# Triangular inverses in a gated delta rule: the second form of each level's inverse made by transposition

## The reference, cut to what matters

```python
L = jnp.where(strict, jnp.einsum('bhncd,bhnsd->bhncs', k_beta, k) * decay, 0.0)
A = jnp.eye(C, dtype=f32) + L
u = lax.linalg.triangular_solve(A, v * beta[..., None], left_side=True, lower=True, unit_diagonal=True)
w = lax.linalg.triangular_solve(A, k_beta * jnp.exp(gc)[..., None], left_side=True, lower=True, unit_diagonal=True)
```

## Time and profile before

| | us |
|---|---|
| median of 3 runs | 4347.78 |
| lowest, highest | 4346.86, 4359.89 |
| the profiled execution | 4345.83 |
| its span, first to last instruction | 4344.0 |
| mean granted TensorE clock | 0.966 of full |

### The profile page before, as it was taken

The page is one execution under the profiler, slowest core; times in us unless marked ns, Lnnn a source line. Parts: engine busy times, 40 slices in busy tenths (PEclk is TensorE's granted clock), DMA queues, the critical chain, the costliest instruction groups (busy, mean ns, idle before and its releaser), DMA issues.

```text
span 4344.0 us, 36733 instructions
## 1 busy us (share of the span) xinstructions
PE 4066.7 (94%) x13837; PEld 2293.4 (53%) x13837; DVE 2045.6 (47%) x3759; ACT 869.9 (20%) x1735; POOL 390.1 (9%) x252
## 2 busy tenths in 40 slices
PE   6998989999999999998998999989998969599999
PEld 3343555555554555544445444456664458556665
DVE  2130530898104456564323298046665055455666
ACT  2111520000113111113133000221112131242111
POOL 1110000344020000000000034100000000100000
PEclk9999999999999999999999999999999979589999
DMA  5552001111112111111210222122222200102222
GB/s 209 194 204 68 1 9 55 58 39 58 39 64 63 59 58 58 58 57 43 78 39 5 78 78 78 58 107 78 97 78 75 69 20 0 48 1 78 97 78 78
DMA packets 124950, 294.51 MB, mean 68 GB/s; under 512 B 5130, under 2 KB 13370, under 8 KB 124800
## 3 DMA queue, kind: packets, MB, share of 16 engines
q1 hardware_dynamic: 107824, 236.58, 15.4%
q0 software_dynamic: 16976, 55.84, 3.8%
HBM read 290.23 MB, written 2.18 MB: 67 GB/s over the span
## 4 chain that ended last, share of the span: by engine, by line
PE 87%; DVE 6%; ACT 3%; DMA 2%; issue 1%; POOL 0%; DVEq 0%; SPq 0%; ACTq 0%
PE psum L357 30%; PE psum L1911 29%; PE psum L1970 14%; PE psum L1905 3%; PE psum L2015 2%; PE psum L1998 1%; DMA sb_rc<-in_ada_b 1%; ACT sb_rc L1670 1%; PE psum L1956 1%; DMA sb_ring<-in_ada_w 1%; PE psum L1021 1%; ACT sb_rb L1670 1%; PE psum L1034 1%; PE psum L1035 1%; PE psum L1999 0%
## 5 line engine op out<-in xcount | busy, mean ns | idle before, releaser
L1911 PE MATMUL psum<-sb_ht,sb_ring 128*128 128x512 f32 (+1 forms) x2448 | 891.7, 526 | 3.7 <-DVE sb_kvt L2298 2.1
L1911 PEld LDWEIGHTS psum<-sb_ht,sb_ring 128*128 128x128 f32 x2448 | 464.0, 190 | 431.2 <-issue 409.9
L2286 DVE SCALAR_TENSOR_TENSOR sb_rc<-sb_rc,sb_vec x960 | 475.6, 572 | 0.0
L1970 PE MATMUL psum<-sb_ring,sb_ht 128*128 128x512 f32 (+1 forms) x1088 | 466.2, 590 | 5.3 <-DVE sb_rc L2330 3.6
L1670 ACT ACTIVATE sb_rc<-psum 128x512 f32<-128x512 f32 (+2 forms) x330 | 167.3, 525 | 1159.1 <-DVE sb_ra L519 308.1
L357 PE MATMUL psum<-sb_ring,sb_rc 128*128 128x512 f32 x868 | 391.8, 593 | 7.5 <-DVE sb_rc L503 7.5
L1970 PEld LDWEIGHTS psum<-sb_ring,sb_ht 128*128 128x128 f32 x1088 | 208.3, 193 | 262.2 <-issue 256.9
L357 PE MATMUL psum<-sb_ht,sb_ring 128*128 128x256 f32 (+1 forms) x1152 | 306.6, 416 | 0.0
L1670 ACT ACTIVATE sb_kvt<-psum 128x512 f32<-128x512 f32 (+2 forms) x197 | 100.0, 533 | 1004.6 <-PE psum L1911 788.0
L1911 PE MATMUL psum<-sb_rc,sb_ring 128*128 128x512 f32 (+1 forms) x768 | 276.6, 522 | 4.3 <-ACT sb_rc L1670 2.5
L357 PEld LDWEIGHTS psum<-sb_ring,sb_rc 128*128 128x128 f32 x868 | 164.5, 190 | 216.6 <-issue 204.3
(11 more groups left out here) (358 smaller groups left out, 4486.1 us busy)
## 6 DMA issues: line engine op xcount, KB each, us to landing
sb_ring<-in_w_in SPq DMA_DIRECT2D x37, 2048.0 KB, 8.0
sb_ring<-in_w_ff SPq DMA_DIRECT2D x32, 2048.0 KB, 8.0
sb_rc<-in_ada_w POOLq DMA_DIRECT2D x20, 2048.0 KB, 8.3
sb_ring<-in_w_ffn SPq DMA_DIRECT2D x16, 2048.0 KB, 7.9
sb_ring<-in_w_out SPq DMA_DIRECT2D x6, 2048.0 KB, 8.1
sb_ring<-in_ada_w SPq DMA_DIRECT2D x4, 2048.0 KB, 12.9
sb_ring<-in_w_gmlp_o SPq DMA_DIRECT2D x4, 2048.0 KB, 8.3
sb_ring<-in_w_attn_o SPq DMA_DIRECT2D x4, 2048.0 KB, 7.9
```

The costliest lines, as they stand in the source:

```text
L1911: last = pe.matmul(bank(b + v, m), ring[:, slot, k, j * P:(j + 1) * P], rhs[:, k, a:a + m], start=k == 0, stop=k == KT - 1)
L1970: last = pe.matmul(bank(4 + g % 4, width), lhs[:, k, i * P:(i + 1) * P], ring[:, slot, k, 0:width], start=k == 0, stop=k == KT - 1)
L2286: step = stt(conv_slot(j, a, m), conv_slot(j + 1, a + k, m), vec[:, j, k:k + 1], conv_slot(j, a, m), op0=ALU.mult, op1=ALU.add)
```

## The change

TensorE no longer makes `xi` by a product. It makes `xit` alone (3 matmuls a unit), and when VectorE has subtracted it, TensorE transposes the new `xit` of the unit before (`turn_back`, 3 transpositions into bank 5 + u % 3, semaphore `s_xt_ps`) and ScalarE copies the result to `xi` (`turned`). The count `s_x0` becomes `s_x_cm` with 40 counts, 8 from the start values and 8 for each of four levels, and the first product of a unit waits for its own unit's count. In the last level nothing is transposed; that level stands outside the loop on TensorE and ScalarE. The waits at the end of each level are gone; VectorE waits once for its own last subtraction, behind the loop.

```diff
-            with act.Fori(0, 5) as level:
-                for u in range(8):
+            def level_evictions(level, last_level):
+
+                def first(u):
                     act.wait_ge(*s_p1_ps.at(0, 8 * level + u + 1))
                     fn(lm[:, u, :, :], bank(u % 2, 384).rearrange("p (h n) -> p h n", h=3)).then_inc(s_p1_sb.sem, 1)
+
+                def turned(u):
+                    act.wait_ge(*s_xt_ps.at(0, 8 * level + u + 1))
+                    fn(xi[:, u, :, :], bank(5 + u % 3, 384).rearrange("p (h n) -> p h n", h=3)).then_inc(s_x_cm.sem, 1)
+
+                first(0)
+                first(1)
+                for u in range(8):
+                    if u + 2 < 8:
+                        first(u + 2)
+                    if u and not last_level:
+                        turned(u - 1)
+                if not last_level:
+                    turned(7)
+
+            with act.Fori(0, 4) as level:
+                level_evictions(level, False)
+            level_evictions(4, True)
...
-            with pe.Fori(0, 5) as level:
+            def level_products(level, last_level):
+
                 def first(u):
                     pe.wait_ge(*s_bt.at(0, 8 * level + u + 1))
+                    pe.wait_ge(*s_x_cm.at(0, 8 * level + u + 1))
                     if u >= 2:
                         pe.wait_ge(*s_p1_sb.at(0, 8 * level + u - 1))
...
+                def turn_back(u):
+                    pe.wait_ge(*s_xx_sb.at(0, 8 * level + u + 1))
+                    pe.wait_ge(*s_x_cm.at(0, 8 * level + u + 6))
+                    for h in range(3):
+                        last = turn(bank(5 + u % 3, P, h * P), xit[:, u, h, :])
+                    last.then_inc(s_xt_ps.sem, 1)
...
-                        pe.matmul(bank(2 + u % 3, P, h * P), xit[:, u, h, :], lm[:, u, h, :], start=True, stop=True)
-                        last = pe.matmul(bank(5 + u % 3, P, h * P), lm[:, u, h, :], xit[:, u, h, :],
+                        last = pe.matmul(bank(2 + u % 3, P, h * P), lm[:, u, h, :], xit[:, u, h, :],
                                          start=True, stop=True)
                     last.then_inc(s_xx_ps.sem, 1)
-                pe.wait_ge(*s_xx_sb.at(0, 8 * level + 8))
+                    if u and not last_level:
+                        turn_back(u - 1)
+                if not last_level:
+                    turn_back(7)
+
+            with pe.Fori(0, 4) as level:
+                level_products(level, False)
+            level_products(4, True)
...
                     dve.wait_ge(*s_xx_ps.at(0, 8 * level + u + 1))
-                    ch_x = tt(xi[:, u, :, :], xi[:, u, :, :], bank(2 + u % 3, 384).rearrange("p (h n) -> p h n", h=3),
-                              ALU.subtract)
-                    tt(xit[:, u, :, :], xit[:, u, :, :], bank(5 + u % 3, 384).rearrange("p (h n) -> p h n", h=3),
+                    tt(xit[:, u, :, :], xit[:, u, :, :], bank(2 + u % 3, 384).rearrange("p (h n) -> p h n", h=3),
                            ALU.subtract).then_inc(s_xx_sb.sem, 1)
-                dve.wait_ge(*s_xx_sb.at(0, 8 * level + 8))
-
+
+            dve.wait_ge(*s_xx_sb.at(0, 40))
             dve.wait_ge(*s_p1_ps.at(0, 40))
```

More of the change, by code:

```diff
@@ L658, in build_program @@
         s_lt_sb = signal("lt_sb", 8)
-        s_x0 = signal("x0", 8)
+        s_x_cm = signal("x_cm", 40)
         s_bt = signal("bt", 40)
@@ L664, in build_program @@
         s_xx_sb = signal("xx_sb", 40)
+        s_xt_ps = signal("xt_ps", 32)
         s_wu_ps = signal("wu_ps", 8)
@@ L1009, in second_pe @@
             pe.wait_ge(*s_qd2.at(0, 1))
-            pe.wait_ge(*s_x0.at(0, 8))
+            pe.wait_ge(*s_x_cm.at(0, 8))
             pe.wait_ge(*s_lt_sb.at(0, 8))
@@ L1304, in second_dve @@
                 ch.note(tt(xit[:, u, :, :], rep(ident[:, :], 3), xit[:, u, :, :], ALU.subtract))
-                tt(xi[:, u, :, :], rep(ident[:, :], 3), xi[:, u, :, :], ALU.subtract).then_inc(s_x0.sem, 1)
-            dve.wait_ge(*s_x0.at(0, 8))
+                tt(xi[:, u, :, :], rep(ident[:, :], 3), xi[:, u, :, :], ALU.subtract).then_inc(s_x_cm.sem, 1)
+            dve.wait_ge(*s_x_cm.at(0, 8))
             dve.wait_ge(*s_lt_sb.at(0, 8))
```

## The result

| | before | after |
|---|---|---|
| median of 4 executions, us | 4347.57 | 4319.89 |
| lowest, highest | 4346.86, 4359.89 | 4319.34, 4321.30 |
| the profiled execution, us | 4345.83 | 4320.28 |
| its span | 4344.0 | 4318.3 |

The ratio is 0.9925, with a 95% interval from 0.9908 to 0.9942. The kernel is faster by more than 0.3%. The medians are 27.7 us apart and the two profiled spans 25.7 us; the ratio takes in the one execution of the kernel before at 4359.89 us and stands for 32.6 us (0.0075 x 4347.57).

A forecast was written before the change was run, and what follows sets the result against it. TensorE was taken to bound the kernel, busy 94% of the span. Terms 26.8 - 10.7 + 6.7 + 0.5 + 2.8 - 0.3 = 25.8 us less gave 4320.0 to 4322.0, stated as 4321 us; range 4316 to 4330.

The forecast's parts named there:

- The sum: Whole kernel: 26.8 - 10.7 + 6.7 + 0.5 + 2.8 - 0.3 = 25.8 us gained, all passed on to the end.
- The records: TensorE in the levels: 240 product records removed (26.8 us), 96 transpositions added (10.7 us), net 16.1 us less.
- changing between the two kinds of record: TensorE, between matmuls and transpositions: claimed to cost nothing where the tile stays 128x128.
- the first rival: Within units: new waits eat 10.7 us (4332), or each change of record kind costs 0.1 us (4327); together 0.12.
- The boundaries: Between levels: each costs 0.73 us beyond counted transpositions where it cost 2.41; 1.68 x 4 = 6.7 us gained.
- What is late next at the boundary is the mask product: Level boundary: after the change the VectorE mask product, not ScalarE, is late next; 1.40 us by the chain's pieces.
- The end: Before the next stage: one subtraction fewer gains 0.5 us; some 0.3 us lost if the loop exit is paid twice.
- The clock: Levels three and five: 1.4 us each lost to a lower clock after idle TensorE, 2.8 us counted as gained.
- The second rival: Levels: transpositions count as idle, the clock falls to half, 34 us slower, 4381 us; chance 0.04.
- The third rival: Later stage: a transfer or fixed event bounds it and the gain is waited away, 4346 us; chance 0.03.
- the step from the sum to the range: Whole kernel: range 4316 to 4330 us, the forecast with a few us of scatter, and the change-of-kind case.

The follow-up runs named there:

- e5_by_matmul: Changed kernel with each transposition made by an fp32 matmul with the identity, two records instead of one; levels 78.4 us, one execution 4344.14 us.
- e6_unrolled: Changed kernel with the level loops of TensorE, VectorE and ScalarE written out; levels 69.1 us, ratio 0.9940 to the kernel before.
- e8_idle: Changed kernel with five more VectorE mask products ahead of each level's first, so TensorE idles at the boundaries; levels 87.3 us.
- e2_waits: Kernel before with both products kept, the waits at each level's end replaced by waits per unit; levels 90.3 us, ratio 0.9981.
- b1_before: Kernel before, unedited, profiled again to catch a long execution; 4360.74 us.
- e1_again: Changed kernel, unedited, timed again in five rounds against the kernel before; median 4324.73 us against 4358.25, ratio 0.9925.
- f2_after: Changed kernel, unedited, timed once more against the kernel before; median 4320.57 us of 6, ratio 0.9938.
- e3_level_waits: Changed kernel with the waits at the end of each level put back; levels 73.9 us, ratio 0.9934 to the kernel before.
- e7_stream: Changed kernel with the five levels as one stream of 40 units, working ahead across boundaries; levels 65.2 us, median 4312.77 us, ratio 0.9928 to the kernel before.
- f1_gap: Changed kernel with two more VectorE operations between its last subtraction and the stage behind the levels; ratio 0.9948 to the kernel before.

## Why the prediction was right and where it was wrong

*The sum was right for the levels.* 25.8 us were forecast, the levels gave 25.92 and the spans differ by 25.7; 4321 was said, 4319.89 is the median. Two of its terms were off by 0.6 to 0.7 us each, in opposite directions, so the close hit of the total is in part luck. Its terms one by one:

- The records: 240 gone and 96 new at the price of the earlier trace rows. A unit takes 0.67 + 0.67 + 0.33 us, 16.1 us in all, and 0.2 more because a transposition is 0.110 us and not 0.1117. So changing between the two kinds of record costs nothing here either. e5_by_matmul shows that a record more is paid in full, so no new wait bounds a unit: the first rival is out.
- The boundaries: 6.7 forecast, 6.0 found: 2.41 and three times 2.38 before, 1.67, 1.60, 1.60 and 1.40 after, of which 4 x 0.67 are the transpositions, counted already. A step that failed is "What is late next at the boundary is the mask product". Where TensorE jumps back it is the last unit's transposition and, behind it, TensorE's own jump, 0.2 to 0.3 us, which the text had not costed; only VectorE's was. Where it does not (the fourth boundary; e6_unrolled, 1.39), the boundary is the forecast's 1.40.
- The end: 0.5 less 0.3 forecast, 0.8 found. From the last record's start to the next stage it was 1.71 us and is 0.92. The loop's exit ahead of the fifth level costs nothing that shows: the fourth boundary is the shortest.
- The clock: 2.8 forecast and found. Together the terms found are 25.9 us. e8_idle shows the dips to come with idle time of 2.4 us, and e2_waits that without the long idle time they are gone even with both products.

*The second rival is out.* With a fifth of the records transpositions, the clock was 1.00 in all levels. The Trainium skill, "TensorE: Matmul & The Clock Gate", Part 4, says that the full clock does not engage for transpositions. If they had counted as idle time here, it was not enough to bring the clock down; the earlier trace rows, where transpositions alone brought it from 0.50 to 1.00, does not agree with that sentence.

*The third rival is out.* The spans differ by what the levels gave, within 0.2 us.

*What failed is the step from the sum to the range.* "The range is 4316 to 4330: the forecast with that scatter" took the scatter of the kernel before for noise around the same 25.8 us, and put a difference between the two kernels' long executions at nothing without a reason. It is more than noise: in b1_before the stage behind the levels runs at half clock, 11.0 us longer, and the changed kernel had no execution 10 us above its lowest in 16. So the ratio stands for 32.6 us where the sum had 25.8. By the ratio, 0.9925, the time is 4315.2 from the median stated, 0.8 below the lower end. The row was there: 4359.89 in the times of before, 12 above the median, against a profile in which that stage has a clock of 1.00. The question of what that execution held was not asked, and the lower end should have had it, some 6 to 10 us lower (an estimate, from the 6 us by which the ratio beats the levels and the 11.0 of the stage) for a kernel that meets it seldom or never. Over the executions of the kernel before in this study, 13 of 48 took 4355 or more, 9 of them beside e1_again, where the ratio was 0.9925; beside f2_after one of eleven was, and the ratio was 0.9938. So what a ratio says of the change moves with how many long executions the kernel before happens to have beside it. That the change itself makes them rarer is argued by counts only: e3_level_waits, e5_by_matmul and e7_stream differ little from the changed kernel and had four, so its none of 16 can be chance.

A slip of the text: forecast and first rival, 0.80 and 0.12, are 0.92 and not 0.91.

What remains open is why the stage falls to half clock in one execution and not in the next. The idle time ahead of it is a candidate, not shown; the moment at which the stage starts is another, and was not tried.

## What to carry to other kernels

A product that only yields the transpose of another product can be a transposition: here half the price on TensorE in fp32, and one copy more on ScalarE. Cost the boundary of a loop by the chain of every engine in it, its jump included, and see whether work can be taken across it: here a stream without boundaries took another 4.5 us off the levels. Where the times of a kernel fall in two heaps, ask for a profile of the upper one before a range is given.

## What the runs showed of the hardware that was not expected

- TensorE can fall from 2.4 to 1.2 GHz while it is busy, and not come back. It did so 1.9 us into the stage of line 1049 (fp32 matmuls of 128x128 on 64 columns of weights, and of 128x64) in b1_before and stayed at 1.2 GHz for the remaining 26 us of it, busy without a break; in other executions of the same code it stayed at 2.4 GHz (17.2 us from first to last record's start, in place of 28.0). TensorE had been idle for 1.4 us ahead of the stage there, for 1.7 in f1_gap, where it fell after 2 us, and for 0.6 in e5_by_matmul, where it fell after 2.7.
- Dips of the clock behind the level boundaries, by TensorE's idle time there: 2.1 us, 10 of 16 boundaries in four profiles of the kernel before; 2.4 us, 4 of 4 (e8_idle); 1.6 us or less, none of 4 in e2_waits, e3_level_waits and the changed kernel each.
- A VectorE operation on 64 partitions takes as long as on 128: four of them 1.97 us in e8_idle, four mask products of the same length 1.96 us in e3_level_waits, 0.47 us start to start.
